# Other short products between the slabs of the first feed-forward layer, and one more wait ahead of a weight load

## The reference

```python
h2 = rms_norm(x, norm_ffn[l])
gu = jnp.einsum('bsd,df->bsf', h2, w_ffn_in[l])            # 1024 -> 2 * 2816
x = x + jnp.einsum('bsf,fd->bsd', jax.nn.silu(gu[..., :D_FF]) * gu[..., D_FF:], w_ffn_out[l])
```

```python
up = causal_dwconv(h @ w_up[l], conv_ffn_w[l])
a, b = jnp.split(up, 2, axis=-1)
x = x + (jax.nn.silu(a) * b) @ w_down[l]
```

## Time and profile before

| what | value |
|---|---|
| median of three runs | 1296.4 us |
| the profiled execution's own time | 1296.4 us |
| its span | 1294.7 us |
| TensorE busy | 1270.2 us (98%) |
| TensorE weight loads busy | 1064.7 us |
| VectorE busy | 893.9 us (69%) |
| ScalarE busy | 588.5 us (45%) |
| TensorE's share of the chain that ended last | 95% |

### The profile page before, as it was taken

The page is one execution under the profiler, slowest core; times in us unless marked ns, Lnnn a source line. Parts: engine busy times, 40 slices in busy tenths (PEclk is TensorE's granted clock), DMA queues, the critical chain, the costliest instruction groups (busy, mean ns, idle before and its releaser), DMA issues.

```text
span 1294.7 us, 17058 instructions
## 1 busy us (share of the span) xinstructions
PE 1270.2 (98%) x6810; PEld 1064.7 (82%) x6810; DVE 893.9 (69%) x1062; ACT 588.5 (45%) x704; POOL 130.6 (10%) x120
## 2 busy tenths in 40 slices
PE   7999999999999999999999999999999999999997
PEld 5777677789999899998888888668888888888876
DVE  6788655887888688887536433658665656668796
ACT  6372672564554445564311322563433333336555
POOL 4003010013222010200000002000300000001020
PEclk9999999999999999999999999999999999999999
DMA  5422101259999497823433332102222222256765
GB/s 168 136 75 88 66 1 59 88 147 179 202 197 179 106 236 230 151 63 113 163 98 98 98 98 98 65 1 74 91 97 97 97 97 97 97 186 104 205 107 137
DMA packets 120708, 151.81 MB, mean 117 GB/s; under 512 B 4170, under 2 KB 93498, under 8 KB 120514
## 3 DMA queue, kind: packets, MB, share of 16 engines
q1 hardware_dynamic: 91906, 108.92, 25.2%
q0 software_dynamic: 28720, 41.96, 19.1%
q10 hardware_dynamic: 16, 0.00, 0.0%
HBM read 148.76 MB, written 2.11 MB: 117 GB/s over the span
## 4 chain that ended last, share of the span: by engine, by line
PE 95%; DVE 2%; ACT 2%; DMA 0%; issue 0%; SPq 0%; ACTq 0%
PE psum L1897 20%; PE psum L1899 20%; PE psum L1898 20%; PE psum L2158 4%; PE psum L2159 4%; PE psum L2160 4%; PE psum L2202 3%; PE psum L2354 3%; PE psum L2204 3%; PE psum L2356 3%; PE psum L2355 3%; PE psum L2203 3%; PE psum L2037 1%; PE psum L2022 1%; PE psum L2268 1%; PE psum L2049 1%
## 5 line engine op out<-in xcount | busy, mean ns | idle before, releaser
L1897 PE MATMUL psum<-act_hi,w_hi 128*128 128x512 f32 x968 | 385.1, 398 | 4.2 <-DVE act_lo L1191 1.7
L1898 PE MATMUL psum<-act_lo,w_hi 128*128 128x512 f32 x968 | 378.6, 391 | 0.0
L1899 PE MATMUL psum<-act_hi,w_lo 128*128 128x512 f32 x968 | 378.5, 391 | 0.0
L778 ACT ACTIVATE w_hi<-raw 128x2048 fp32r<-128x2048 f32 (+1 forms) x104 | 167.0, 1606 | 396.5 <-PE psum L1899 370.5
L1182 DVE TENSOR_TENSOR w_lo<-raw,w_hi 128x2048 fp32r<-128x2048 f32 (+1 forms) x104 | 199.4, 1918 | 63.2 <-ACT w_hi L778 63.2
L1897 PEld LDWEIGHTS psum<-act_hi,w_hi 128*128 128x128 f32 x968 | 181.8, 188 | 48.7 <-issue 6.5
L1899 PEld LDWEIGHTS psum<-act_hi,w_lo 128*128 128x128 f32 x968 | 181.8, 188 | 41.2
L1898 PEld LDWEIGHTS psum<-act_lo,w_hi 128*128 128x128 f32 x968 | 181.9, 188 | 39.5 <-issue 1.7
L2202 PE MATMUL psum<-part_hi,w_hi 128*128 128x256 f32 x308 | 86.3, 280 | 0.0
L2204 PE MATMUL psum<-part_hi,w_lo 128*128 128x256 f32 x308 | 85.9, 279 | 0.0
L2203 PE MATMUL psum<-part_lo,w_hi 128*128 128x256 f32 x308 | 85.9, 279 | 0.0
(11 more groups left out here) (334 smaller groups left out, 2270.2 us busy)
## 6 DMA issues: line engine op xcount, KB each, us to landing
raw<-in_w_in SPq DMA_DIRECT2D x30, 1024.0 KB, 5.1
raw<-in_w_up SPq DMA_DIRECT2D x22, 1024.0 KB, 5.0
xz<-in_w_ffn_in POOLq DMA_DIRECT2D x24, 512.0 KB, 6.5
raw<-in_w_ffn_in SPq DMA_DIRECT2D x22, 512.0 KB, 5.3
x_buf<-in_w_ffn_out POOLq DMA_DIRECT2D x6, 1024.0 KB, 9.2
x_buf<-in_w_down POOLq DMA_DIRECT2D x6, 1024.0 KB, 9.8
raw<-in_w_out SPq DMA_DIRECT2D x4, 1024.0 KB, 4.9
xz<-in_w_ffn_in SPq DMA_DIRECT2D x8, 512.0 KB, 5.4
```

What stands on the lines that cost most here:

```text
L778: A(w_at(w_hi, s, h, n - h), home(s, n)[:, h:n], ACT.Copy).then_inc(w_hi_ready, 1)
L1897: mm(dst, stationary[0], moving[0], start=first, stop=False)
L1898: mm(dst, stationary[0], moving[1], start=False, stop=False)
L1899: return mm(dst, stationary[1], moving[0], start=False, stop=last)
```

## The change

The list `SHORT` becomes a table of 14 places, each with a word of letters: f is one fp32 column, b one bf16 column, F one fp32 matmul of 128 columns, B one of 128 bf16 columns, R one of 128 columns in the fp32r type that the real products use. Small letters are counted, capital letters are used once (FF is one F). The letter order of execution is f, b, F, B, R. The new places are the slabs (p0, i) and (p3, i-1) for i = 3 to 9. The short products ahead of (p3, 9), (p6, 9) and both down products are gone. SyncE has one more wait: it loads part 6 of the first down product only after TensorE has done parts 0 to 2.

```diff
-SHORT = [("p0", 3), ("p3", 9), ("p6", 9)]
+SHORT = {("p0", 3): "f", ("p3", 2): "b", ("p0", 4): "ff", ("p3", 3): "bb", ("p0", 5): "F", ("p3", 4): "B", ("p0", 6): "R",
+         ("p3", 5): "FF", ("p0", 7): "fff", ("p3", 6): "bbb", ("p0", 8): "fb", ("p3", 7): "Fb", ("p0", 9): "bR", ("p3", 8): "Ff"}
...
                 if s == S_DOWN + 6:
                     sp.wait_ge(w_lo_ready, S_DOWN)
+                    sp.wait_ge(slab_done, S_DOWN + 3)
...
-            def two_columns(bank):
-                for _ in range(2):
-                    mm(psum[:, bank, 0:1], ident_bf[:], ident_bf[:, 0:1], start=True, stop=True)
...
+            def short_products(how, bank):
+
+                for _ in range(how.count("f")):
+                    mm(psum[:, bank, 0:1], ident[:], ident[:, 0:1], start=True, stop=True)
+                for _ in range(how.count("b")):
+                    mm(psum[:, bank, 0:1], ident_bf[:], ident_bf[:, 0:1], start=True, stop=True)
+                if "F" in how:
+                    mm(psum[:, bank, 0:P], ident[:], ones[:], start=True, stop=True)
+                if "B" in how:
+                    mm(psum[:, bank, 0:P], ident_bf[:], ident_bf[:], start=True, stop=True)
+                if "R" in how:
+                    mm(psum[:, bank, 0:P], neg_ones[:], neg_tri[:], start=True, stop=True)
...
-                if (kind, i) in SHORT:
-                    two_columns(UP_BANK[kind])
+                short_products(SHORT.get((kind, i), ""), UP_BANK[kind])
...
-                if n == 0:
-                    two_columns(4)
```

## The result

The changed kernel took 1306.09 us (median of six runs, 1305.61 to 1306.57) against 1296.68 us of the kernel before in the same runs. The ratio is 1.0074, with an interval from 1.006 to 1.0086: slower by 9.4 us. I had forecast 1302.0 and a range up to 1304.9. The profiled execution took 1306.76 us, its span is 1305.0, 10.3 us longer than before.

The account below looks back on a forecast made before the run. The prediction took TensorE, busy in 1270.2 of 1294.7 us, to bound the kernel. From 1296.4 us it added 3.0 for the words net of removed pairs, 2.6 for slow slabs and 0 for the wait: 1302.0 us, range 1297.9 to 1304.9.

Parts of the forecast that it names:

- What bounds the kernel: TensorE is busy in 1270.2 of 1294.7 us, so a change there counts nearly in full.
- The price of the words: Short products at the 14 places cost 3.8 us on TensorE, five removed pairs save 0.8: net +3.0 us.
- The spacing behind each new place: Of the 49 slabs from (p0, 3) on, all fast before, half turn slow: +2.6 us.
- rival (b): Nearly all 49 slabs turn slow, from the first b or bb on: 1304.6 us, chance 0.12.
- The new wait: SyncE's later load of part 6 in the first down product costs nothing, with 6 and 4 us to spare.
- Rival (d): The late load stalls TensorE at part 6 by 1 to 3 us: 1303 to 1305 us, chance 0.05.
- The removed pairs: At (p3, 9), (p6, 9) and both down products the spacing stays; only the pairs' own time is saved.
- Rival (c): The first down product runs fast without the pairs before it, 4.1 us less: 1295.3 or 1297.9 us, chance 0.11.
- The sum: For the whole kernel, 1296.4 + 3.0 + 2.6 + 0 = 1302.0 us.

Follow-up runs that it names:

- e6: The changed kernel without its SyncE wait and with only its first four words, f, b, ff, bb: 1297.8 us, ratio 0.9996.
- e13: The kernel before with the pair at (p0, 3) alone, the other four pairs removed, no new words or wait: 1295.46 us, ratio 0.9994.
- e2: The kernel before with the new SyncE wait alone added: 1300.01 us, ratio 1.0026.
- e5: The kernel before with only the pair at (p3, 9) removed: 1292.72 us median, ratio 0.9969.
- e15: The kernel before without the pair at (p3, 9), with bb (p1, 2), bR (p0, 3), fb (p3, 2): 1292.84 us, ratio 0.9964.
- e3: The kernel before without the pair at (p0, 3), the other four pairs kept: 1298.04 us, ratio 1.0013.
- e4: The changed kernel without its SyncE wait and with the word bb at all 14 places: 1302.78 us, ratio 1.0047.
- e8: The changed kernel, wait kept, with adding DMAs of parts 9 to 11 held until part 7's load has landed: 1308.09 us, ratio 1.007.
- e10: The kernel before without the pair at (p3, 9), F at (p1, 2), nine words misplaced into the first down product: 1297.1 us, one run.
- e12: The kernel before without the pair at (p3, 9), bb at (p1, 2), fb for bb at (p0, 3): 1292.95 us median, ratio 0.9984.
- e1: The changed kernel without its new SyncE wait: 1305.37 us, ratio 1.0065.

## Why the prediction was wrong, step by step

- **What bounds the kernel**: right. TensorE's two spacings, 113.3 and 117.8 ns, the words and its waits explain the whole difference. Both spacings, and both of the 512-column matmuls, stand in windows with a clock of 1.00 and TensorE busy throughout, so neither the clock nor a wait sets them apart.
- **The price of the words**: right, 3.7 us against 3.8, as were the single prices.
- **The spacing behind each new place**: the first of two steps that failed, a mis-sized term. I took "half of the slabs slow: +2.6 us"; it was 42 of 49, 4.5 us. What stood behind the half was wrong too: a word doesn't leave the spacing to chance, but takes each of seven states to a fixed one. The trace of before shows five pairs, and these have different results because they met S1, A3, A1 and S3; by the group view I could have seen the states, but not what 12 other words do to them. I also read the pair at (p3, 9) as one that "left" the spacing slow. It came behind a fast stretch, and without it (e6, e13) the slabs there are fast by themselves: that pair made them slow. My rival (b) was nearest in time, 1304.6, but not in its condition: the first bb, at (p3, 3), gave the fast spacing.
- **The new wait**: "Cost nothing, with 6 and 4 us to spare" failed, a term put at nothing that cost more than the spacing's error of 1.9 us: 2.6 us in the trace, and 3.6 us alone by the medians of e2, with a lower granted clock in nine of its ten runs. I gave the load half of 386 GB/s beside an adding DMA, 5.4 us; it took 12.1. The half itself was near: SyncE's queue had 48.3% of the DMA engines' time from 484 to 497. But I counted part 6 alone, and that queue moved 1.92 MB in these 13 us, since part 7's load ran beside part 6's and didn't wait for it; and 1.92 MB in 13 us are 148 GB/s, less than the half of 386. The rows of before gave a warning: where many loads are adding ones, from 299.62 to 430.18, the DMA share is 0.94 at only 186 GB/s, while plain loads reach 386. Rival (d) had the mechanism, with 0.05. Either failed step alone would have left the time within the range (1303.9 or 1304.6); together they put it outside.
- **The removed pairs**: right for this kernel, which arrived at (p3, 9) in A1 and not in A3. In a kernel with a fast stretch, the removal at (p3, 9) is worth some 4 us (e5, in six of its nine runs). Rival (c) was a true mechanism of the kernel and not of this change.
- **The sum**: 3.0 + 2.6 + 0 should have been 2.9 + 4.5 + 2.6, 10.0, for 10.3 measured in the spans and 9.4 in the medians.

Open is what the states are in the hardware: no run here shows what keeps the phase. Open is also what sets the arrival (of the 17 profiles ten reach the first 256-column slab in S1, four in S2, two fast and one in S3), and whether e15 is free of times near 1301 or was lucky in six. And no run has tried a word in the second down product.

## What to carry to other kernels

Read the spacing and the phase slab by slab, from the starts and the group view, before pricing a short product that is put in or taken out. Here one kind of matmul had two spacings, 113.3 and 117.8 ns, and the pair bb turned a slow stream fast at one place (all 49 slabs behind (p0, 3) in the kernel before, slow in e3 without it) and a fast one slow at another ((p3, 2) in e4), and each time the new spacing stayed up to the next interruption. When a load is moved to a later time, count what else the DMA engines carry then, the loads behind it in its own queue too: the same 1.92 MB of SyncE's queue took 13 us where the adding DMAs had 52.6% of the engines' time, and 8 us where they had 26.2% (e8). The GB/s alone didn't show the room that was left: the share was 0.94 at 186 GB/s and 1.04 at 386. And before a result that shows no effect is believed, check in the trace that the inserted instructions stand where they were meant to (e10).

## What the runs showed of the hardware that I had not expected

- TensorE's start-to-start spacing in the fp32r streams of these profiles had few, stable values: for 256 columns 113.3 ns (the kernel before from 299.62 to 430.18) and 117.8 (its down product), for 512 columns 228.9 (by the starts, from 430.2 to 441) and 233.3 (e12 from 257.6 to 274), each at a granted clock of 1.00. With the weights moving, 512 columns ran at 233.3 in every profile; with the activations moving nearly always at 228.9, but not always: at 233.3 in e12, and in the kernel before from 69.6 to 75.0 as well (398 ns in all three lines). The slow spacing costs 5.2 us over the 49 slabs and 4.1 us over the down product, worked out from 4.45 ns a matmul.
- In the changed kernel a single fp32 matmul of one column cost 0.22 us (fff, 0.66 us for three), as much as one of 128 columns (F, 0.22), while one of 128 columns in fp32r cost 0.10 (R).
- A plain load of 1 MB took 12.1 us beside adding DMAs and a second plain load (the changed kernel, 484.62 to 496.69), and 6.6 us where the adding ones were held (e8).
- The granted clock fell for some 4 us soon after a TensorE stall of over 2 us in e2 (0.57 from 507 to 511, and 0.50 from 508 to 510) and e8 (0.57 from 514 to 518), but not after a stall of 2.2 us in the changed kernel (1.00 from 505 to 510), and in e1 it fell in attention (0.50 from 842 to 844). The one in e1 cost 1.7 us.
- The same kernel can have two times, 1292.7 and 1301.2 in e5. The profile at 1301.8 has no wait and no lower clock that explains it, but 117.8 ns in all 49 slabs and in the down product; that the executions near 1292.7 differ by the phase alone is inferred from their time.
